# Twelve down tiles move from the dense rows into the gate rounds

## The reference

```
q = (hf @ w_query)                        # 8 heads, two halves of 128
s1, s2 = q against sub_keys1, sub_keys2   # 128 scores each
v1, i1 = top_k(s1, 16); v2, i2 = top_k(s2, 16)
idx, gates = top 16 of the 256 sums v1+v2 (expert i1*128+i2), softmax
act = gelu(hb . expert_down[idx])         # per token, 128 chosen experts
out = sum(gates * act * expert_up[idx])
```

## Time and profile before

| | us |
|---|---|
| median of 3 runs | 2844.78 (2844.61 to 2851.24) |
| the profiled execution | 2850.61 |
| its span | 2848.9 |
| gate rounds, from the first group to the last | about 756 to 915 |
| rows with a down and an up tile | about 936 to 1604 |
| rows with an up tile alone | about 1604 to 1803 |

### The profile page before, as it was taken

One profiled execution on the slowest core, in us unless ns is written; L12 is line 12 of the kernel. 1 busy time (PEld: TensorE's weight loads), 2 busy tenths in 40 slices (PEclk: granted clock), 3 DMA queues, 4 the chain that ended last, 5 costly groups with the idle time before them and its releaser, 6 DMA issues.

```text
span 2848.9 us, 35887 instructions
## 1 busy us (share of the span) xinstructions
PE 2671.0 (94%) x12743; PEld 2132.9 (75%) x12743; DVE 1800.6 (63%) x3271; ACT 942.8 (33%) x1217; POOL 850.2 (30%) x546
## 2 busy tenths in 40 slices
PE   4999899999777999999999999999998999899997
PEld 2455345699756899999999887699877877588875
DVE  5843755799898787878888898740118532460532
ACT  2324222333466333323233222443333233332221
POOL 2100001155300334444344322143322234244442
PEclk8999999999999999999999999999999999899999
DMA  9511344333234898899888899233724432132221
GB/s 337 178 56 59 105 140 155 128 125 118 96 166 165 303 315 309 313 319 321 313 312 308 291 306 314 99 107 101 123 86 143 148 114 87 59 96 95 91 96 59
DMA packets 191363, 502.55 MB, mean 176 GB/s; under 512 B 30801, under 2 KB 79985, under 8 KB 189217
## 3 DMA queue, kind: packets, MB, share of 16 engines
q1 hardware_dynamic: 141680, 317.30, 33.7%
q0 software_dynamic: 49584, 184.04, 18.3%
HBM read 454.42 MB, written 46.86 MB: 176 GB/s over the span
## 4 chain that ended last, share of the span: by engine, by line
PE 64%; issue 16%; DVE 12%; POOL 5%; DMA 1%; DVEq 1%; ACT 1%; POOLq 0%; ACTq 0%
PE psum L1624 18%; PE psum L1611 14%; PE psum L1919 14%; PE psum L544 6%; PE psum L529 6%; POOL l_r L849 5%; DVE arena L1967 3%; DVE arena L1964 2%; DVE look_oh L1964 2%; DVEq L1967 1%; DVE arena L1971 1%; PE psum L1351 1%; PE psum L1926 1%; DVE arena L2310 1%; DVE arena L2311 1%
## 5 line engine op out<-in xcount | busy, mean ns | idle before, releaser
L874 ACT ACTIVATE arena<-psum 128x512 f32<-128x512 f32 (+8 forms) x474 | 319.4, 685 | 1165.4 <-PE psum L1611 385.6
L1964 DVE TENSOR_TENSOR arena<-arena 128x384 f32<-128x384 f32 (+7 forms) x399 | 306.1, 773 | 540.8 <-ACT arena L874 270.4
L849 POOL TENSOR_TENSOR l_r<-arena,l_r 128x1024 fp32r<-128x1024 f32 x144 | 351.2, 2440 | 663.3 <-ACT l_r L488 663.3
L1624 PE MATMUL psum<-e_r,e_r 128*128 128x512 f32 x2304 | 540.4, 391 | 3.2 <-DVE e_r L1964 3.2
L1611 PE MATMUL psum<-e_r,e_r 128*128 128x384 f32 x2048 | 525.9, 337 | 8.5 <-issue 4.0
L1624 PEld LDWEIGHTS psum<-e_r,e_r 128*128 128x128 f32 x2304 | 432.3, 188 | 91.0 <-DVE e_r L1964 3.6
L874 ACT ACTIVATE e_r<-arena 128x1024 fp32r<-128x1024 f32 x256 | 270.3, 1057 | 364.0 <-PE psum L1624 334.8
L1611 PEld LDWEIGHTS psum<-e_r,e_r 128*128 128x128 f32 x2048 | 371.4, 189 | 20.7 <-issue 6.9
L1611 PE MATMUL psum<-e_r,l_r 128*128 128x384 f32 x1024 | 344.4, 336 | 0.0
L833 POOL DMA_INDIRECT arena<-in_up,arena x128 | 163.5, 1277 | 279.0 <-DVE arena L2436 144.4
L833 POOL DMA_INDIRECT arena<-in_down_rows,arena x128 | 164.0, 1282 | 251.0 <-DVE arena L1971 123.7
(11 more groups left out here) (231 smaller groups left out, 3383.1 us busy)
## 6 DMA issues: line engine op xcount, KB each, us to landing
arena<-in_down SPq DMA_DIRECT2D x128, 512.0 KB
arena<-in_up SPq DMA_DIRECT2D x128, 512.0 KB, 7.0
arena<-in_w_ada POOLq DMA_DIRECT2D x48, 512.0 KB, 7.0
scratch_gates<-arena SPq DMA_DIRECT2D x12, 2048.0 KB, 6.3
arena<-scratch_gates SPq DMA_DIRECT2D x32, 768.0 KB
arena<-in_w_in SPq DMA_DIRECT2D x44, 512.0 KB, 3.7
arena<-in_w_query SPq DMA_DIRECT2D x16, 512.0 KB, 3.7
arena<-in_w_glu SPq DMA_DIRECT2D x16, 512.0 KB, 3.7
```

What stands on the lines that cost most here:

```text
L849: nc.gpsimd.tensor_tensor(rr(lo, 1024, "l"), reg(RING + q % NSLOT * SLOT, 1024), rr(hi, 1024, "l").bitcast(F32), ALU.subtract).then_inc(S[ ...
L874: do(sc.activation(out, in_, f, **kw), sem)
L1624: last = mm(bank(2 * tt_ + hf), rr(w__ + tt_ * P, P), rr(x__ + hf * 512, 512), start=(first and n == 0), stop=(final and n == 2))
L1964: do(v.tensor_tensor(out, a, b, op), sem)
```

## The change

A new number, ES = 12. Twelve down tiles (those of rows 48 to 59) are computed inside the gate rounds, one for each chunk: behind each group's one-hot products TensorE does 3 of the tile's 24 matmuls. Their gelu results have no place in ACTB yet; they go to a small ring (EOUT, 3 entries at PV) and from there to memory (`early`, 12 x 192 KB). During the first 12 dense rows they are loaded back, each into the ACTB entry that `weigh` of that row has just finished with. These first 12 rows now do an up tile alone; 68 rows with both follow, then 48 with an up tile alone, as before. Order and row number differ now, so `row_of` and `order_of` translate.

The low parts of all down tiles from the gate rounds on are made by VectorE: one `low_d` ahead of the rounds, one in the middle of each chunk, and those of the four tiles behind the rounds after them. VectorE's one loop of 48 turns becomes 24 loops of two turns each, written out. The sparse operations are spread anew: one for each of the first 12 rows, 49/17 for each of the next 68, one for each of the last 48. GpSimd's first gather waits for the `early` stores too.

```diff
-EB, EG = 44, 4
+EB, ES, EG = 44, 12, 4
+EO = EA + ES
-ED = NKEY - EA
+ED = NKEY - EO
+        EOUT = PV
         def sparse_from(q):
-            return q * 13 // 5 if q < ED else ED * 13 // 5 + (q - ED)
+            if q < ES:
+                return q
+            return ES + (q - ES) * 49 // 17 if q < ES + ED else ES + ED * 49 // 17 + (q - ES - ED)
...
 # SyncE
             for c in range(NGC):
                 sp.wait_ge(S["g_evac"], S.base("g_evac") + GB + 8 * (c + 1))
                 sp.dma_start(io["gates"][c], reg(STG[c % 2], GCHUNK * P)).then_inc(S[f"g_stored{c % 2}"], 16)
+                load_down(EB + NSLOT + c)
+                sp.wait_ge(S["e_g"], S.base("e_g") + 2 + EB + c + 1)
+                sp.dma_start(io["early"][c], reg(EOUT + c % 3 * TD, TD)).then_inc(S[f"early_out{c % 3}"], 16)
...
-            for n in range(EB + NSLOT, EA + NSLOT):
+            for n in range(EB + ES + NSLOT, EO + NSLOT):
                 load_down(n)
+            for n in range(3):
+                sp.wait_ge(S[f"early_out{n}"], S.base(f"early_out{n}") + 16 * (ES // 3))
             for q in range(NKEY - NSLOT):
-                if EA + NSLOT + q < NKEY:
+                if q < ES:
+                    sp.wait_ge(S["e_w"], S.base("e_w") + q + 1)
+                    sp.dma_start(reg(ACTB + q * TD, TD), io["early"][q]).then_inc(S["h_back"], 16)
+                elif EA + NSLOT + q < NKEY:
                     load_down(EA + NSLOT + q)
                 load_up(NSLOT + q)
...
 # GpSimd
-            for n in range(EA):
+            for n in range(EB):
...
             pool.wait_ge(S["g_stored1"], S.base("g_stored1") + 16 * (NGC // 2))
+            for n in range(3):
+                pool.wait_ge(S[f"early_out{n}"], S.base(f"early_out{n}") + 16 * (ES // 3))
...
 # ScalarE
             def gelu(n):
                 wait("e_u", n + 1)
-                act_(reg(ACTB + n % EA * TD, TD), bank(6 + n % 2, TD), ACT.Gelu, "~e_g")
+                row = row_of(n)
+                if EB <= n < EB + ES:
+                    c = n - EB
+                    if c >= 3:
+                        wait(f"early_out{c % 3}", 16 * (c // 3))
+                    act_(reg(EOUT + c % 3 * TD, TD), bank(6 + n % 2, TD), ACT.Gelu, "~e_g")
+                else:
+                    act_(reg(ACTB + row % EA * TD, TD), bank(6 + n % 2, TD), ACT.Gelu, "~e_g")
...
 # at the end of each chunk's eight evacuations
+                gelu(EB + c)
+                hi_d(EB + c + 2)
-            for n in range(EB, EA):
+            for n in range(EB + ES, EO):
                 gelu_early(n)
-                if n < EA - 1:
+                if n < EO - 1:
                     hi_d(n + 2)
             wait("g_mm", GB + TD // 4)
             hi_u(0)
...
 # TensorE
-            with pe.Fori(0, TD // 4 // GB) as i:
-                for u_ in range(GB):
+            with pe.Fori(0, NGC // NSLOT) as i:
+                for x in range(8 * NSLOT):
+                    r, u_ = x // 8, x % GB
...
                     last.then_inc(S["g_mm"], 1)
+                    if x % 8 == 0:
+                        pe.wait_ge(S["d_loB"], S.base("d_loB") + i * NSLOT + (r + 1))
+                        pe.wait_ge(S["e_g"], S.base("e_g") + i * NSLOT + (EB + r + 1))
+                    down_part(draw(r), DHI + (r % 2) * 1024, 6 + r % 2, x % 8 * 3, x % 8 * 3 + 3)
...
+            for q in range(ES):
+                pe.wait_ge(S["u_lo"], S.base("u_lo") + q + 1)
+                pe.wait_ge(S["e_w"], S.base("e_w") + q + 1)
+                up_unit(q % 2, UHI + (q % 2) * 1024, uraw(q % NSLOT), q == 0)
+            with pe.Fori(0, ED // NSLOT) as i:
                 for r in range(NSLOT):
                     both(i, r)
...
 # VectorE
+            low_d(EB)
             wait("slots_T", 3)
-            with tn.loop(TD // 4 // GB, b_hot=GB) as i:
+            for c in range(2 * NGC):
+                with tn.loop(4 // GB, b_hot=GB) as i:
...
+                if c % 2 == 0:
+                    low_d(EB + c // 2 + 1)
+            for n in range(EB + ES + 1, EO):
+                low_d(n)
...
             do(v.memset(reg(YS, 1024), 0.0))
-            low_d(EA)
+            low_d(EO)
             low_u(0)
             for q in range(-1, NKEY):
                 if q + 1 < NKEY:
                     n = q + 1
                     weigh(n)
-                    if 0 <= q and EA + 1 + q < NKEY:
+                    if ES <= q and EA + 1 + q < NKEY:
                         low_d(EA + 1 + q)
```

More of the change, by code:

```diff
@@ L1083, in gelu_early @@
             def gelu_early(n):
+                row = row_of(n)
                 for tb in range(4):
[L1085 removed]
+                    if (row + 1) * TD > SC - ACTB + 2048 * tb >= row * TD:
                         wait("sc_free", tb + 1)
@@ L1119, in _ @@
             for q in range(NKEY):
-                if EA + q + 1 < NKEY:
+                if ES <= q and EA + q + 1 < NKEY:
                     hi_d(EA + q + 1)
@@ L1123, in _ @@
                     hi_u(q + 1)
-                if EA + q < NKEY:
+                if ES <= q and EA + q < NKEY:
                     wait("e_w", q + 1)
@@ L1648, in _, with both @@
                     last.then_inc(S["g_mm"], 1)
+                    if x % 8 == 0:
+                        pe.wait_ge(S["d_loB"], S.base("d_loB") + i * NSLOT + (r + 1))
+                        pe.wait_ge(S["e_g"], S.base("e_g") + i * NSLOT + (EB + r + 1))
+                    down_part(draw(r), DHI + (r % 2) * 1024, 6 + r % 2, x % 8 * 3, x % 8 * 3 + 3)
             for r in range(EG):
-                pe.wait_ge(S["d_loA"], S.base("d_loA") + EB + r + 1)
-                pe.wait_ge(S["e_g"], S.base("e_g") + EB + r + 1)
+                pe.wait_ge(S["d_loB"], S.base("d_loB") + ES + r + 1)
+                pe.wait_ge(S["e_g"], S.base("e_g") + EB + ES + r + 1)
                 down_unit(draw(r), DHI + (r % 2) * 1024, 6 + r % 2)
             pe.wait_ge(S["g_evac"], S.base("g_evac") + TD // 4 + GB)
-            def both(i, r, first=False):
-                pe.wait_ge(S["d_loB"], S.base("d_loB") + i * NSLOT + (r + 1))
-                pe.wait_ge(S["e_g"], S.base("e_g") + i * NSLOT + (EA + r + 1))
+            def both(i, r):
+                pe.wait_ge(S["d_loB"], S.base("d_loB") + i * NSLOT + (EO - EB + r + 1))
+                pe.wait_ge(S["e_g"], S.base("e_g") + i * NSLOT + (EO + r + 1))
                 down_unit(draw(r), DHI + (r % 2) * 1024, 6 + r % 2)
[L1660 to L1666, removed]
+                pe.wait_ge(S["u_lo"], S.base("u_lo") + i * NSLOT + (ES + r + 1))
+                pe.wait_ge(S["e_w"], S.base("e_w") + i * NSLOT + (ES + r + 1))
+                up_unit(r % 2, UHI + (r % 2) * 1024, uraw(r))
+            for q in range(ES):
[3 more added lines that the diff above has]
+            with pe.Fori(0, ED // NSLOT) as i:
                 for r in range(NSLOT):
@@ L2406, in low_d @@
                    ALU.subtract, "~d_loB")
+            low_d(EB)
+            wait("slots_T", 3)
+            for c in range(2 * NGC):
+                with tn.loop(4 // GB, b_hot=GB) as i:
+                    for u_ in range(GB):
+                        n = 4 * c + u_
+                        wait("g_mm", i * GB + (n + 1))
+                        tt(three(OA + u_ * 512, 4, P), bc(con("iota").unsqueeze(1), [P, 4, P]),
+                           bc(A[:, bass.ds(i * (4 * GB) + (I1T + 4 * n), 4)].unsqueeze(2), [P, 4, P]), ALU.is_equal, FREE)
+                        for t in range(4):
+                            ts(reg(OB + u_ * 512 + t * P, P), con("iota"), A[:, bass.ds(i * (4 * GB) + (I2T + 4 * n + t), 1)],
+                               A[:, bass.ds(i * (4 * GB) + (GT + 4 * n + t), 1)], ALU.is_equal, ALU.mult,
+                               "~b_hot" if t == 3 else FREE)
+                if c % 2 == 0:
+                    low_d(EB + c // 2 + 1)
+            for n in range(EB + ES + 1, EO):
+                low_d(n)
             def low_u(n):
@@ L2419, in weigh @@
                     wait("e_y", n - 1)
-                wait("e_g", 2 + n + 1)
+                if EA <= n < EO:
+                    wait("h_back", 16 * ES)
+                else:
+                    wait("e_g", 2 + order_of(n) + 1)
                 a3 = reg(ACTB + n % EA * TD, TD).rearrange("p (c t) -> p c t", c=NGC)
@@ L2840 @@
     io["out"] = nc.dram_tensor("out_0", (D, T), F32, kind="ExternalOutput").ap()
-    for n, shape in (("gates", (NGC, P, GCHUNK * P)), ("spill", (P, KT * T)), ("u_d", (8, P, T2)),
+    for n, shape in (("gates", (NGC, P, GCHUNK * P)), ("early", (ES, P, TD)), ("spill", (P, KT * T)), ("u_d", (8, P, T2)),
                      ("s5w", (8, P, 1024)), ("s5v", (8, P, 1024)), ("s5cs", (8, P, 1056)), ("s5k", (8, S5H, 1024))):
```

27 lines of the change are left out of this document (13 added, 14 removed).

## The result

The changed kernel takes 2815.5 us (median of 4 runs, 2814.0 to 2816.1) where the kernel before took 2846.1 beside it: a ratio of 0.9882, interval 0.9866 to 0.9898. That is 30.6 us less; 23.8 were forecast, and the time lies inside the range of 2810 to 2838. Its profiled execution has 2815.15 us and a span of 2813.5.

What follows compares the result with a forecast made beforehand. VectorE was taken to bound the gate rounds and TensorE the dense rows with both tiles. Terms -50.2 + 14.6 + 1.0 + 1.2 + 7.6 + 2.0 = -23.8 us gave 2821.0 us, range 2810 to 2838.

Steps and rivals of the forecast that it cites:

- 12 down tiles out of the rows: Dense rows: twelve down tiles at 4.18 us each leave TensorE, which never idles there; 50.2 us less.
- `low_d`, table load, loops: the rounds: Gate rounds: growth of 14.6 us for twelve low parts on VectorE, 1.0 for the table load, 1.2 for loop heads.
- hand-over: Between gate rounds and dense rows: TensorE's wait and slow start before up tile 0 grow by 7.6 us, between 2.6 and 13.
- traffic in the first 80 rows: Dense rows with up tile alone and with both: DMA near 348 GB/s costs 2 us, between 0 and 7.
- the last 48 rows: Final dense rows, an up tile alone in each: expected as before, with no term in the sum.
- The heads of loops: Gate rounds, VectorE: entering 24 small loops instead of one costs 0.1 us for each of 12, 1.2 us.
- The table load: Gate rounds, ScalarE: the 1.28 us load moves to chunk 0 and adds 1 us, between 0 and 1.3.
- The order of the lists: Hand-over: up tile 0's operands are made after the down tile's low part, so TensorE waits at least 2.6 us more.
- 0.72 MB more in the queue: Hand-over, SyncE's queue: an extra down tile and last `early` store in front, at about 340 GB/s, cost 2.1 us.
- earlier gathers: Hand-over: GpSimd's five gathers start some 2 us earlier, against the load TensorE waits for, costing about 1.3 us.
- The slow start: Hand-over: an up tile at half clock after the wait costs up to 4.1 us over, 1.6 more than before.
- bound by transfers: Rival, dense rows: DMA sets the pace; hard form at 309 GB/s about 2867 us, milder at 325 2836 us; chance 0.07.

## Why the prediction was right, and where it was off

The mechanism held at each step: VectorE stayed the bound of the rounds, groups kept 1.63 us, the down matmuls fit, the rows kept 8.31 us, the gain came from the rows. All terms but one erred on the same side, so the range was not hit because errors cancelled. Eight us of the stretch's 31.8 were not forecast, and the terms share them out (rounded, so that the last column adds up to within 0.1):

| term | forecast | measured |
|---|---|---|
| 12 down tiles out of the rows | -50.2 | -50.7 |
| `low_d`, table load, loops: the rounds | +16.8 | +14.6 |
| hand-over | +7.6 | +3.2 |
| traffic in the first 80 rows | +2.0 | 0 |
| four tiles behind the rounds | 0 | 0 |
| the last 48 rows | 0 | +1.2 |
| sum | -23.8 | -31.8 |

*The rows.* Up tiles that follow each other take 4.08 us each (138.78 us for 34 in the chain), not the 4.12 they take between down tiles: 0.5 us.

*The rounds.* A `low_d` occupies VectorE for 1.13 to 1.14 us where I took its own 1.22 (1 us in all). The heads of loops cost nothing where I took 1.2. The table load cost nothing either, where I took 1.0: VectorE never waits behind it. Its last wait in the rounds ended twelve us before it:

```profile
762.49 0.69 DVE L2007 TENSOR_TENSOR arena<-cst,arena 128x512 f32<-128x512 f32 x1 [0.94 <-PE psum L1683]
...
774.52 1.28 ACT L900 ACT_TABLE_LOAD   x1 [0.16 <-ACT arena L900]
```

That wait belongs to the first groups. TensorE's granted clock is 0.50 from 755.75 to 762.00, and the eight products of a group took 1.91 us there in place of 1.16; before has 0.50 there too. With down matmuls in between VectorE waited 0.74 + 0.94 us, where it had waited 0.74 + 0.40: 0.5 us that no term of mine had. The three down matmuls behind the last group's products add 0.3. So 13.6 + 0.5 + 0.3 of the 14.6 are accounted for.

*The hand-over.* This is the term that was mis-sized most, by 4.4 us. The order of the lists was read rightly: `e_w(0)` comes one chain after the down tile's load, and that cost 2.75 us where I had 2.6. But I added 2.1 us for 0.72 MB more in the queue and 1.3 for earlier gathers, and the load came only 1.0 us later, counted from the last store. The store took 7.3 us in place of 6.3, and from there to the load it was 10.7 us both times. The gathers started 1.9 us earlier counted from the landing of the stores, about as I had it, and 0.7 to 0.9 counted from the last store; but the run that held them back shows them worth 0.3 us at most, not 1.3. Pricing them by equal shares was wrong here. The Trainium skill ("DMA: Bandwidth & Descriptors", Issuing engines are not separate DMA queues) says that both share the 16 engines; that gives no price, and nothing here speaks against it. The slow start cost 51.20 - 12 x 4.08 = 2.2 us, about what it cost before (2.5), where I had 1.6 more. Why 0.72 MB cost 1.0 us and not 2 can be read in part from the windows between the landing of the stores and the load, before and in the changed kernel:

```profile
922.70:933.40 10.70, 9.15 (x53) 8.64 (x51) 0.00 (x0) 1.93 (x3) 7.54 (x7) 1.00 0.93 283
```

```profile
937.70:948.30 10.60, 8.51 (x50) 8.19 (x48) 2.14 (x2) 2.04 (x3) 5.36 (x5) 1.00 1.05 335
```

Before, the engines had room here (283 GB/s) and in the 6.3 us of the stores (share 0.79, now 0.90 over 7.3 us). The added bytes went in part into that room. I had priced them as if there were none.

*Traffic.* No loss in the 68 rows, though the DMA share was 0.92, and none in the 12 that the slow start does not cover. The 348 GB/s, bytes divided by busy share, was a wrong limit: at a share of 1.00 the same rows passed 375, and 407 was the end. The rival "bound by transfers" was weaker than its 0.07; its hard form also adds up to about 2869 us and not to 2867.

*The last 48 rows.* Their 1.2 us more are no cost of the change: they vary by about 3 us for another reason, below.

## What to carry to other kernels

Work for an idle engine can be put into a loop that another engine paces, if it is cut so fine that it fits into each turn; double buffers give a fraction of a turn, and the average idle time of the loop says nothing. Before giving an operation to an engine that idles, look at which one it runs beside: GpSimd's idle time was worth less than nothing next to VectorE's tensor_scalar. When work is taken out of a stage, spread anew what hid behind it, and look at what the first unit of the next stage waits for: here the order of three lists was worth another 7 to 8 us at the hand-over, and about 6 in the total time.

## What the runs showed that I had not expected

A GpSimd tensor_tensor over 128x1024 held up a tensor_scalar of VectorE until it was over (2.40 us for the one, 3.18 for the group of four in place of 1.1).

The busy share of the DMA engines is not linear in bytes: 0.92 at 328 GB/s, 1.00 at 375, 1.03 at 407, in the same 68 rows.

The last 12 up tiles vary by 2.8 us. They follow a wait of TensorE for an up tile. TensorE's rows there, in the changed kernel and in the one with the down tile loaded first:

```profile
1719.63 15.60 PE L1660 MATMUL psum<-e_r,e_r 128*128 128x512 f32 x55 [3.11 <-DVE e_r L2007]
```

```profile
1714.48 49.26 PE L1661 MATMUL psum<-e_r,e_r 128*128 128x512 f32 x216 [2.23 <-DVE e_r L2008]
```

After 3.11 us idle the 12 up tiles took 52.1 us, after 2.23 they took 49.3. It looks as if the longer wait brought the slower start, but the other runs don't bear that out: with two added copies a row the wait was 2.23 us again and the 12 tiles took 50.9, with the down tile in one lump it was 2.73 and they took 49.3, and before has 3.18 and 50.9. What differs is the granted clock of the first 8.2 us behind the wait, here in the changed kernel, with the added copies and with the lump:

```profile
1719.60:1727.80 8.20, 8.17 (x23) 6.48 (x24) 5.68 (x8) 0.86 (x1) 1.95 (x2) 0.62 0.78 239
```

```profile
1719.40:1727.60 8.20, 8.19 (x29) 6.62 (x30) 6.73 (x9) 1.06 (x1) 1.95 (x2) 0.79 0.79 231
```

```profile
1771.10:1779.30 8.20, 8.20 (x36) 6.81 (x37) 8.13 (x11) 1.06 (x1) 2.02 (x2) 1.00 0.89 276
```

So part of the start ran at 1.2 GHz in the first two and none in the third. What decides that is not shown. These 2.8 us come and go between kernels with no edit near them.
